# Two fused transformer layers: the up projections multiply X scaled by feature only, the token factor follows in PSUM, the shift rides in two extra columns

## The reference, cut to what matters

```python
mod = silu(c) @ ada_w + ada_b            # six vectors of 1024
x = x + gt1 * rmsnorm(mix @ w_o, mix_post_g)   # second layer: x + gate_a * (mix @ w_o)
h = rmsnorm(x, ffn_pre_g) * (1.0 + sc2) + sh2
u = causal_dwconv(h @ w_up, ffn_conv_w, ffn_conv_b)   # 5632 columns, 3 taps over tokens
u_gate, u_val = split(u, 2)
f = (silu(u_gate) * u_val) @ w_down
x = x + gt2 * rmsnorm(f, ffn_post_g)     # second layer: x + gate_f * f
```

## Time and profile before

| | us |
|---|---|
| three timed runs | 1050.90, 1052.35, 1052.53 (median 1052.35) |
| profiled execution | 1054.07 |
| its span | 1052.3 |
| TensorE busy / weight loads | 1027.0 / 969.1 |
| GpSimd busy | 690.0 |
| ScalarE busy | 623.8 |
| VectorE busy | 556.7 |

### The profile page before, as it was taken

One profiled execution on the slowest core, in us unless ns is written; L12 is line 12 of the kernel. 1 busy time (PEld: TensorE's weight loads), 2 busy tenths in 40 slices (PEclk: granted clock), 3 DMA queues, 4 the chain that ended last, 5 costly groups with the idle time before them and its releaser, 6 DMA issues.

```text
span 1052.3 us, 23216 instructions
## 1 busy us (share of the span) xinstructions
PE 1027.0 (98%) x8537; PEld 969.1 (92%) x8537; DVE 556.7 (53%) x1165; ACT 623.8 (59%) x1121; POOL 690.0 (66%) x306
## 2 busy tenths in 40 slices
PE   7999999999999999999999999999999999999998
PEld 5999999988799989999999899997667699999998
DVE  3577725579974455555522641396476735444400
ACT  4556864477773567666645557735565556666642
POOL 2597899811269866988798387780031076988795
PEclk9999999999999999999999999999999999999999
DMA  9988788655547874777587289866201043666463
GB/s 378 386 306 285 273 304 301 239 184 197 164 156 256 276 250 138 263 238 243 191 295 253 107 290 358 320 225 214 73 26 55 2 140 128 213 199 187 164 217 113
DMA packets 62616, 226.43 MB, mean 215 GB/s; under 512 B 6960, under 2 KB 8272, under 8 KB 61264
## 3 DMA queue, kind: packets, MB, share of 16 engines
q1 hardware_dynamic: 61344, 221.23, 60.6%
q10 hardware_dynamic: 1200, 4.23, 1.4%
HBM read 224.35 MB, written 1.08 MB: 214 GB/s over the span
## 4 chain that ended last, share of the span: by engine, by line
PE 75%; issue 9%; POOL 9%; DVE 4%; ACT 3%; POOLq 0%; ACTq 0%; DVEq 0%
PE psL L553 69%; POOL WL L505 9%; PE psO L553 3%; PE psS L553 2%; PE psL L1092 1%; ACT psL L1689 1%; ACT WH L1155 1%; ACT R L1273 0%; DVE X L2055 0%; DVE psL L2054 0%; DVE sm L2288 0%; PE psS L966 0%; PE psS L1036 0%; ACT R L1704 0%; DVE sm L2287 0%
## 5 line engine op out<-in xcount | busy, mean ns | idle before, releaser
L505 POOL TENSOR_TENSOR WL<-ring,WH 128x1024 fp32r<-128x1024 f32 (+1 forms) x282 | 670.7, 2396 | 234.5 <-ACT WH L1155 185.1
L553 PE MATMUL psL<-HR,WH 128*128 128x256 f32 (+1 forms) x3096 | 513.6, 278 | 2.0 <-DVE HR L1800 1.2
L553 PEld LDWEIGHTS psL<-HR,WH 128*128 128x128 f32 (+1 forms) x3096 | 452.8, 187 | 7.6 <-issue 4.8
L553 PE MATMUL psL<-HR,WL 128*128 128x256 f32 x1536 | 396.3, 277 | 0.0
L1155 ACT ACTIVATE WH<-ring 128x1024 fp32r<-128x1024 f32 (+1 forms) x210 | 216.4, 1042 | 106.6 <-PE psL L553 76.2
L553 PEld LDWEIGHTS psL<-HR,WL 128*128 128x128 f32 x1536 | 275.1, 188 | 0.0
L553 PE MATMUL psL<-RR,WH 128*128 128x256 f32 x1356 | 207.6, 279 | 2.9 <-DVE RR L1985 1.3
L553 PEld LDWEIGHTS psL<-RR,WH 128*128 128x128 f32 x1356 | 186.6, 188 | 4.5 <-issue 2.9
L553 PE MATMUL psL<-RR,WL 128*128 128x256 f32 x672 | 145.8, 278 | 0.3 <-POOL WL L505 0.3
L2083 DVE SCALAR_TENSOR_TENSOR CT<-psL,par,CT 128x254 f32<-128x254 f32 (+1 forms) x176 | 80.8, 480 | 107.0 <-ACT CT L1467 101.9
L1458 ACT ACTIVATE WH<-ring 128x1024 fp32r<-128x1024 f32 (+1 forms) x88 | 92.9, 1058 | 71.4 <-PE psL L553 62.8
(11 more groups left out here) (274 smaller groups left out, 1112.4 us busy)
## 6 DMA issues: line engine op xcount, KB each, us to landing
ring<-wts SPq DMA_DIRECT2D x285, 512.0 KB, 4.2
adaring<-ada_w SPq DMA_DIRECT2D x80, 512.0 KB, 4.8
R<-ada_w SPq DMA_DIRECT2D x8, 1024.0 KB, 16.3
ring<-wts SPq DMA_DIRECT2D x16, 384.0 KB, 3.6
R<-cum_dram ACTq DMA_DIRECT2D x8, 512.0 KB, 4.2
R<-wts SPq DMA_DIRECT2D x8, 512.0 KB, 6.9
...
```

The lines of the kernel that those rows point to most:

```text
L505: nc.gpsimd.tensor_tensor(WL[:, k, 0:n], ring[:, k, 0:n], WH[:, k, 0:n].bitcast(F32), SUB).then_inc(lo_done, 1)
L553: return nc.tensor.matmul(out, lhsT, rhs, start=start, stop=stop)
```

## The change

It does six things.

1. The operand of both up stages is GH and GL, the high and low parts of X·lead, with the feature's factors only. A tile is 258 columns, two pad columns and 256 tokens, and tiles stand 272 floats (1088 bytes) apart. The pad columns hold −shift. All matmuls of both up stages are 258 columns wide.
2. The token factor RS is applied behind the product: VectorE, for each unit, makes a bias from pad column 0 (`BCOL` = bank[:, 0]·(minus the sum of the taps) + conv bias, one column, two factors of the partition) and then multiplies bank[:, 2:258] by RS in PSUM. ScalarE's begin waits for both (new semaphore `f_scaled`) and takes its bias from BCOL. The conv instructions are all 256 wide and read the bank one or two columns earlier, so that the pads stand where the zeros ahead of the sequence were.
3. At the boundary o1 to up1, `up_tiles` issues the three joint units tile pair by tile pair, interleaved with the stat products; no wait for the second root stands ahead of them, and most fillers go. VectorE's and ScalarE's orders of add, operand, squares and low part are written out anew.
4. At o2 to up2, X·lead goes to psO in o2's loop (`gained`), ScalarE copies it to GH, VectorE makes GL; TensorE issues tiles 0 to 3, the sum of squares, tiles 4 to 7, without fillers or a wait for the root.
5. In up1 the ada_step of a pair moves from behind the pair to between the scaling of its first bank and the wait for that bank's begin. In the first pair of each stage the two `next_high` come after both begins.
6. New small instructions: `tap_sums` (two VectorE instructions a layer), `shift_pads` (ScalarE) and `low_pads` (VectorE). Both up stages' `make_h` and `make_hh` go (2 x 16 VectorE and 2 x 8 ScalarE instructions). No DMA is added, removed or moved.

The core of the diff (the rest renames arguments or passes `width` on):

```diff
@@ -230,6 +232,10 @@
+GH, GL = region(HR, 0, a=8, b=TILE2), region(RR, 11904, a=8, b=TILE2)
+NWS = CD[:, :, :].rearrange("p a b -> p (a b)")
+BCOL = csil
@@ -379,6 +386,9 @@
+def gained(m):
+    return psO[:, m % 2, 0:T]
@@ -699,6 +709,22 @@
+    g_hi, g_lo = (lambda k: GH[:, k, 0:T2]), (lambda k: GL[:, k, 0:T2])
+    def up_tiles(name, base, tiles):
+        u0, q0 = PLAN.at[name][1], PLAN.q(name)
+        for k in tiles:
+            pe.wait_ge(h_ready, base + k + 1)
+            for c in range(3):
+                if k == 0:
+                    bank_wait(u0 + c)
+                    split_wait(q0 + c)
+                s = (q0 + c) % SLOTS
+                last = triple(psL[:, (u0 + c) % 4, 0:T2], WH[:, s, k * P:(k + 1) * P], WL[:, s, k * P:(k + 1) * P],
+                              g_hi(k), g_lo(k), k == 0, k == 7)
+                if k == 7:
+                    last.then_inc(lin_done, 1)
@@ -836,12 +862,19 @@
     stat_of_sums("stat_o1", 1)
     fill(u0, 6)
     pe.wait_ge(rs_ready, 6)
-    fill(u0, 5)
-    stat("stat_ffn1", sq_at, 8, base=13)
     fill(u0, 6)
-    pe.wait_ge(rs_ready, 7)
-    fill(u0, 4)
-    linear8("up1", 0, 44, h_hi, h_lo, from_count(h_ready, 8), 3, 5, True)
+    pe.wait_ge(pad_lo, 1)
+    up_tiles("up1", 8, (0, 1))
+    out = scratch("stat_ffn1")
+    for part in range(3):
+        for k in (2 * part, 2 * part + 1):
+            stat_block(out, k, 8, sq_at, 13)
+        if part < 2:
+            up_tiles("up1", 8, (2 * part + 2, 2 * part + 3))
+    for k in (6, 7):
+        stat_block(out, k, 8, sq_at, 13)
+    up_tiles("up1", 8, (6, 7))
+    linear8("up1", 0, 44, g_hi, g_lo, None, 3, 5, True, T2)
@@ -1121,13 +1154,11 @@
     linear8("o2", 2, 6, o2_hi, o2_lo, late=6)
-    u0 = PLAN.at["up2"][1]
-    fill(u0, 7)
+    pe.wait_ge(pad_lo, 2)
+    up_tiles("up2", 24, range(4))
     stat_of_sums("stat_ffn2", 3)
-    fill(u0, 7)
-    pe.wait_ge(rs_ready, 12)
-    fill(u0, 4)
-    linear8("up2", 0, 44, h_hi, h_lo, from_count(h_ready, 24), 3, 5, True)
+    up_tiles("up2", 24, range(4, 8))
+    linear8("up2", 0, 44, g_hi, g_lo, None, 3, 5, True, T2)
@@ -1179,6 +1210,10 @@
+    def shift_pads(shift):
+        A(GH[:, :, 0:2], shift.unsqueeze(2).to_broadcast([P, KD, 2]), ACT.Copy, scale=-1.0).then_inc(pad_hi, 1)
@@ -1435,16 +1472,33 @@
-    scale_and_square("o1", MIX, lead[:, 8:16], 0, SQ_O1)
+    scale_and_square("o1", MIX, lead[:, 8:16], 0, SQ_O1, mod[:, 24:32])
...
-    square_x(0, SCRATCH["stat_o1"])
+    def up_operand(j):
+        act.wait_ge(x_ready, j + 1)
+        A(GH[:, j, 2:T2], X[:, j, :], ACT.Identity, scale=lead[:, 16 + j:17 + j]).then_inc(hh_ready, 1)
+    def up_squares(j):
+        act.wait_ge(x_ready, j + 2)
+        A(SQ[:, j * T:(j + 2) * T], wide(X[:, j:j + 2, :]), ACT.Square).then_inc(sq_ready, 2)
+    up_operand(0)
+    up_operand(1)
+    up_squares(0)
+    for j in (2, 4):
+        up_operand(j)
+        up_operand(j + 1)
+        up_squares(j)
+    up_squares(6)
+    up_operand(6)
+    up_operand(7)
...
-    make_hh(mod[:, 24:32], 8)
...
@@ -1464,11 +1518,13 @@
                     act.wait_ge((f_silu, f_prod)[b], base + j - 1 + it)
-                A(CT[:, 2 * slot + b, :], psL[:, u % 4, 0:T], ACT.Identity,
+                act.wait_ge(f_scaled, 4 * (base + j) + 2 * b + 2 + it * 4)
+                A(CT[:, 2 * slot + b, :], psL[:, u % 4, 2:T2], ACT.Identity,
                   scale=par[:, bass.ds(w0 + 2 * 44 + b * KF + j + it, 1)],
-                  bias=par[:, bass.ds(b0 + b * KF + j + it, 1)]).then_inc(f_begun, 1)
-                if j == 0:
-                    next_high(b)
+                  bias=BCOL[:, 2 * slot + b:2 * slot + b + 1]).then_inc(f_begun, 1)
+            if j == 0:
+                next_high(0)
+                next_high(1)
@@ -1732,6 +1788,8 @@
         if m >= 1:
...
             A(square_place(m - 1, 2), X[:, m - 1, :], ACT.Square).then_inc(sq_ready, 1)
+            act.wait_ge(t_ready, 16 + m)
+            A(GH[:, m - 1, 2:T2], gained(m - 1), ACT.Copy).then_inc(hh_ready, 1)
@@ -2056,32 +2116,95 @@
+    def tap_sums(name):
+        tap = lambda n: pv(name, 44 * n, 44)
+        st.link(V.scalar_tensor_tensor(NWS[:, 0:44], tap(0), -1.0, tap(1), MUL, SUB))
+        st.link(V.tensor_tensor(NWS[:, 0:44], NWS[:, 0:44], tap(2), SUB))
+    def low_pads(shift, use):
+        dve.wait_ge(pad_hi, use)
+        V.scalar_tensor_tensor(GL[:, :, 0:2], shift.unsqueeze(2).to_broadcast([P, KD, 2]), -1.0,
+                               GH[:, :, 0:2].bitcast(F32), MUL, SUB).then_inc(pad_lo, 1)
+    tap_sums("fconv_w")
     for m in range(8):
         add_squares(m, 5)
...
+        if m == 1:
+            low_pads(mod[:, 24:32], 1)
...
     dve.wait_ge(rs_ready, 6)
...
-    add_normed(MIX, "stat_o1", PLAN.at["up1"][1], 0)
-    dve.wait_ge(rs_ready, 7)
-    make_h(mod[:, 24:32], lead[:, 16:24], RS[:, 1, :], 8)
-    def ffn(name, wname, base, between):
+    root = sbank("stat_o1")[:, 0:T]
+    part = psL[:, (PLAN.at["up1"][1] + 3) % 4, :].rearrange("p (a b) -> p a b", b=T)
+    def scaled_part(j, n, slot):
+        st.link(V.tensor_tensor(part[:, slot:slot + n, :], MIX[:, j:j + n, :],
+                                root.unsqueeze(1).to_broadcast([P, n, T]), MUL))
+    def add_part(j, n, slot):
+        V.tensor_tensor(X[:, j:j + n, :], X[:, j:j + n, :], part[:, slot:slot + n, :], ADD).then_inc(x_ready, n)
+        dve.wait_ge(x_ready, j + n)
+    def up_low(j):
+        dve.wait_ge(hh_ready, 8 + j + 1)
+        V.scalar_tensor_tensor(GL[:, j, 2:T2], X[:, j, :], lead[:, 16 + j:17 + j], GH[:, j, 2:T2].bitcast(F32),
+                               MUL, SUB).then_inc(h_ready, 1)
+    scaled_part(0, 1, 0)
+    add_part(0, 1, 0)
+    scaled_part(1, 1, 1)
+    add_part(1, 1, 1)
+    up_low(0)
+    up_low(1)
+    scaled_part(2, 2, 0)
+    add_part(2, 2, 0)
+    scaled_part(4, 2, 0)
+    up_low(2)
+    up_low(3)
+    add_part(4, 2, 0)
+    scaled_part(6, 2, 0)
+    up_low(4)
+    up_low(5)
+    add_part(6, 2, 0)
+    dve.sem_inc(s_free[SCRATCH["stat_o1"] % 2], 1)
+    up_low(6)
+    up_low(7)
+    def ffn(name, wname, bname, rs, base, between):
...
-        w0 = PAR[wname][0]
-        def conv(j, slot, it=0, uses=0):
+        w0, b0 = PAR[wname][0], PAR[bname][0]
+        def scale(j, slot, b, it):
+            u = u0 + 2 * j + b
+            bank = psL[:, u % 4, :]
+            dve.wait_ge(lin_done, u + 1 + it * 2)
+            V.tensor_scalar(BCOL[:, 2 * slot + b:2 * slot + b + 1], bank[:, 0:1], NWS[:, bass.ds(b * KF + j + it, 1)],
+                            par[:, bass.ds(b0 + b * KF + j + it, 1)], MUL, ADD).then_inc(f_scaled, 1)
+            V.tensor_tensor(bank[:, 2:T2], bank[:, 2:T2], rs, MUL).then_inc(f_scaled, 1)
+        def conv(j, slot, it=0, uses=0, fill=None):
...
             for back in (1, 2):
                 for b in range(2):
                     if back == 1:
+                        if j > 0 or b == 0:
+                            scale(j, slot, b, it)
+                        if j == 0 and b == 0:
+                            scale(j, slot, 1, it)
+                        if fill and b == 0:
+                            fill()
                         dve.wait_ge(f_begun, 2 * base + 2 * j + b + 1 + it * 2)
-                    dst = CT[:, 2 * slot + b, back:T]
+                    dst = CT[:, 2 * slot + b, :]
...
-                        dst, psL[:, us[b] % 4, 0:T - back],
+                        dst, psL[:, us[b] % 4, 2 - back:T2 - back],
...
                     if back == 1:
@@ -2109,17 +2232,13 @@
         product(0, 0)
         with st.repeat(2, 16) as i:
             for q in range(8):
-                conv(2 + q, q % 2, i * 8, i * 4)
+                conv(2 + q, q % 2, i * 8, i * 4, between and (lambda: between(q, i)))
                 product(1 + q, (1 + q) % 2, i * 8)
                 product_low(q, q % 2, i * 8)
-                if between:
-                    between(q, i)
         for j in range(18, KF):
-            conv(j, j % 2)
+            conv(j, j % 2, fill=between and (lambda: between(j - 2, None)))
             product(j - 1, (j - 1) % 2)
             product_low(j - 2, j % 2)
-            if between:
-                between(j - 2, None)
         product(21, 1)
         product_low(20, 0)
         product_low(21, 1)
@@ -2399,6 +2519,11 @@
+    def up2_low(m):
+        dve.wait_ge(hh_ready, 24 + m + 1)
+        V.tensor_tensor(GL[:, m, 2:T2], gained(m), GH[:, m, 2:T2].bitcast(F32), SUB).then_inc(h_ready, 1)
@@ -2408,15 +2533,23 @@
                                    ).then_inc(lin_free[u % 4], 1)
...
-            if sq_base is not None and m >= 1:
-                add_squares(m - 1, sq_base)
+            if sq_base is not None:
+                if m >= 2:
+                    dve.wait_ge(h_ready, 24 + m - 1)
+                V.tensor_scalar(gained(m), X[:, m, :], lead[:, 8 + m:9 + m], None, MUL).then_inc(t_ready, 1)
+                if m == 1:
+                    low_pads(mod[:, 24:32], 2)
+                if m >= 1:
```

(23 more changed lines are left out.)

28 lines of the change are left out of this document (16 added, 12 removed).

## The result

The changed kernel takes 1060.64 us (median of 4 runs, 1059.74 to 1062.26) against 1051.95 us for the kernel before on the same chip: ratio 1.0075, 95% interval 1.006 to 1.009. It is **slower by 0.75%** (the two medians alone give 0.83%); I had forecast 1051.5, no difference, in a range of 1046.0 to 1058.5. The profiled execution took 1059.74 us, 5.67 more than the one of before; the medians differ by 8.7, three more, which no trace here assigns; the last experiments touch on it.

The account below looks back on a forecast made before the run. The prediction took TensorE's own work to bound the up stages. Boundaries −8.2, wider products +1.6 and scaled banks +5.8 summed to −0.8, moving the median from 1052.35 to 1051.5 us, range 1046.0 to 1058.5.

Parts of the forecast that it names:

- I take the slope: Up-stage products: two more columns cost 0.415 ns each, 0.83 ns a product, 1.76 us over 2112 products.
- My upper bound of 6.7 ns: Up-stage products: at most the surplus over 256 columns is paid once more per product, 14.1 us in all.
- The column-step rival: Up stages: 258 columns or wider tile spacing costs 6.7 ns a product; −8.2 + 14.0, 1058 us; chance 0.10.
- The boundaries: Before both up stages: joint units end earlier without the root wait, gaining 3.1 and 5.1 us, together −8.2.
- The chain: Up-stage scaling through VectorE and ScalarE: 5.59 us a pair in up2, mean 5.72 in up1, against TensorE's 5.48.
- my +5.8 us: TensorE waits caused by the scaling chain: 1.2 us in up2, 3.2 in up1, 1.4 at down1's start.
- The hidden edits: tap_sums, shift_pads and low_pads fit where VectorE and ScalarE wait in o1 and o2; otherwise 1 us at a boundary.

Follow-up runs that it names:

- e2: Kernel before with late and looped units of both up stages 258 columns wide, tiles still 1024 bytes apart: 1068.69 us, ratio 1.0147.
- e5: Kernel before, up-stage tiles 1088 bytes apart, tokens at tile start (first stage) or 8 bytes in (second): 117.9 and 119.9 ns a product.
- e6: Kernel before, first up stage's PSUM banks used from byte 8, second's late and looped products 254 columns wide: 113.0 and 118.1 ns a product.
- e11: Changed kernel with TensorE's order of work at both boundaries put back as before: 1072.51 us, ratio 1.0186.
- e7: Changed kernel with 256-column products from tiles 1024 bytes apart again, shift columns stored elsewhere and not multiplied: 1055.20 us, ratio 1.0014.
- e8: Changed kernel with unscaled operand only in each up stage's first 12 units, H made meanwhile for the others: 1067.31 us, ratio 1.0151.

## Why the prediction was wrong

**The failed step: "I take the slope".** I put two more columns at +0.83 ns, 1.76 us in all; the traces show 119.7 against 113.3 in the loops, about 6.4 ns, or 13.5 us over 2112 products. From the joint units' end to the first down product each stage went from 112.2 to 118.65 us (401.60 to 513.80, now 399.06 to 517.71), 12.9 us for the two, where my sum had 1.6. My upper bound of 6.7 ns had the size right and I gave it 0.10. What misled me was to read the 6.7 ns above 256 columns as a fixed cost that any width pays once, and to price a width off rows of another kind (plain fp32, 192 and 512 columns). e2, e5 and e6 show that 113.3 is a special case, and that the change left it twice over, by width and by distance; each alone costs 5 to 8 ns in the table, both together 6.5. Why TensorE has this special case no run shows. (The plain fp32 rows also have two records to a product, so their 0.83 ns a column was that of half a product.)

**The column-step rival is what happened**; it named width or distance, at 6.7 ns. It gave −8.2 + 14.0 = +5.8; on the profiled execution 1054.07 + 5.8 = 1059.9, against 1059.74. The parts agree as well: 8.0 gained at the boundaries, 12.9 lost outside the joint units, and 0.7 that already stood at o1's end make 5.6 of the spans' 5.65; the slow down stage is the first before and the second after, so it cancels. On the median it gave 1058, 2.6 below the 1060.64 measured; the spans differ by 5.65 and the medians by 8.7, and the drawn pace of single stages (one down stage is 2.4 us longer at the slow one, 65.24 against 62.89) has the size to make that difference, which is argued, not shown.

**The boundaries were right.** 3.2 and 4.8 us against my 3.1 and 5.1, with products 6 ns dearer than I had. e11 shows that they count: taking the early start away costs more than they gained.

**The chain was sized right and cost nothing.** I had 5.59 and 5.85 us a pair, the trace 5.65 and 5.83; the one-column instruction took 0.19 of spacing (442.40 to 442.59), as estimated. But my +5.8 us compared it with a TensorE pair of 5.48; the real one is 5.75. The two errors do not add: the slower engine hides the chain. They partly cancel instead, which is luck: without the 5.8 us of waits that never came my forecast would have been 5.8 us further off. e7 takes the cover away and shows waits of the kind that I forecast in the first up stage, 1.54 us at the down stage among them (I had said about 2).

**The hidden edits** stayed hidden. The first timeline row after o1's end shifts by 0.7 us (381.32, was 380.64), and part of that stood there before any edited line. The Trainium skill, "SBUF — State Buffer", section "Who interferes with whom", states that a VectorE instruction with two SBUF inputs contends with a GpSimd instruction that reads SBUF: e8 agrees with it, 1.61 and 1.72 us beside GpSimd's low parts for what takes 0.41 while GpSimd is idle.
